# Feed-forward gate and up in a two-block transformer kernel: activations standing against 512 moving weight columns, or weight tiles standing against 512 moving activation columns

## The reference

```python
def rms_norm(x, g):
    y = xf * lax.rsqrt(jnp.mean(xf * xf, axis=-1, keepdims=True) + RMS_EPS)
    return (y * g).astype(x.dtype)

def swiglu(x, w_gate, w_up, w_down):
    return (jax.nn.silu(x @ w_gate) * (x @ w_up)) @ w_down

# first block, once before the mixer and once behind it
f1 = swiglu(rms_norm(x, ffn1_pre_g[l]), ffn1_w_gate[l], ffn1_w_up[l], ffn1_w_down[l])
x = x + FFN_RESIDUAL_WEIGHT * rms_norm(f1, ffn1_post_g[l])
# second block
x = x + (jax.nn.silu(h2 @ w_ffn_gate[l]) * (h2 @ w_ffn_up[l])) @ w_ffn_down[l]
```

## Time and profile before

| | |
|---|---|
| median of three runs | 1033.18 us (1032.8 to 1033.62) |
| the profiled execution, its own time | 1033.55 us |
| span of its trace | 1031.8 us |
| TensorE busy | 1024.5 us, 99% of the span |
| TensorE weight loads busy (beside matmuls) | 849.1 us, 82% |
| VectorE busy | 631.9 us, 61% |
| ScalarE busy | 473.0 us, 46% |
| GpSimd busy | 71.6 us, 7% |
| weights read from HBM | 177.15 MB, 174 GB/s over the span |

### The profile page before, as it was taken

One profiled execution on the slowest core, in us unless ns is written; L12 is line 12 of the kernel. 1 busy time (PEld: TensorE's weight loads), 2 busy tenths in 40 slices (PEclk: granted clock), 3 DMA queues, 4 the chain that ended last, 5 costly groups with the idle time before them and its releaser, 6 DMA issues.

```text
span 1031.8 us, 13503 instructions
## 1 busy us (share of the span) xinstructions
PE 1024.5 (99%) x5002; PEld 849.1 (82%) x5002; DVE 631.9 (61%) x651; ACT 473.0 (46%) x550; POOL 71.6 (7%) x85
## 2 busy tenths in 40 slices
PE   9999999999999999999999999999999999999998
PEld 6888888888878888888888888888888888888887
DVE  6554455765677654454665488876877675445453
ACT  5534345555465534344544442345437354434432
POOL 1000000120100000000010003262000000000000
PEclk9999999999999999999999999999999999999999
DMA  9655556664224555565746653335435646555541
GB/s 307 232 194 189 191 187 211 197 203 128 99 83 163 168 199 185 181 200 183 246 129 199 197 170 97 111 121 164 147 109 193 202 165 205 189 191 188 196 170 41
DMA packets 116665, 178.78 MB, mean 173 GB/s; under 512 B 5641, under 2 KB 73489, under 8 KB 116497
## 3 DMA queue, kind: packets, MB, share of 16 engines
q1 hardware_dynamic: 115808, 174.82, 51.4%
q10 hardware_dynamic: 304, 1.70, 0.6%
q0 software_dynamic: 512, 1.71, 0.6%
HBM read 177.15 MB, written 2.63 MB: 174 GB/s over the span
## 4 chain that ended last, share of the span: by engine, by line
PE 97%; DVE 1%; DMA 1%; issue 0%; ACT 0%; SPq 0%; ACTq 0%; DVEq 0%
PE gu L518 15%; PE gu L522 14%; PE gu L521 14%; PE acc L518 11%; PE acc L522 11%; PE acc L521 11%; PE tp L518 3%; PE tp L522 3%; PE tp L521 3%; PE acc L888 2%; PE tp L658 1%; PE gu L765 1%; PE acc L747 1%; PE acc L777 1%; PE tp L561 1%; DMA raw<-in_up 1%
## 5 line engine op out<-in xcount | busy, mean ns | idle before, releaser
L1568 DVE TENSOR_TENSOR wlo<-raw,whi 128x2048 fp32r<-128x2048 f32 x149 | 346.4, 2328 | 182.6 <-ACT whi L1070 181.8
L1070 ACT ACTIVATE whi<-raw 128x2048 fp32r<-128x2048 f32 x150 | 286.3, 1912 | 141.7 <-PE acc L522 92.8
L518 PE MATMUL gu<-whi,act_hi 128*128 128x512 f32 x592 | 234.8, 397 | 0.1
L522 PE MATMUL gu<-whi,act_lo 128*128 128x512 f32 x592 | 231.0, 390 | 0.0
L521 PE MATMUL gu<-wlo,act_hi 128*128 128x512 f32 x592 | 230.6, 390 | 0.0
L522 PEld LDWEIGHTS gu<-whi,act_lo 128*128 128x128 f32 x592 | 111.1, 188 | 23.7
L518 PEld LDWEIGHTS gu<-whi,act_hi 128*128 128x128 f32 x592 | 111.2, 188 | 23.0 <-DVE act_lo L1594 0.5
L521 PEld LDWEIGHTS gu<-wlo,act_hi 128*128 128x128 f32 x592 | 111.3, 188 | 21.9
L518 PE MATMUL acc<-whi,hT_hi 128*128 128x512 f32 x240 | 93.7, 390 | 0.0
L522 PE MATMUL acc<-whi,hT_lo 128*128 128x512 f32 x240 | 93.4, 389 | 0.0
L521 PE MATMUL acc<-wlo,hT_hi 128*128 128x512 f32 x240 | 93.4, 389 | 0.0
(11 more groups left out here) (275 smaller groups left out, 1342.7 us busy)
## 6 DMA issues: line engine op xcount, KB each, us to landing
raw<-in_w_in SPq DMA_DIRECT2D x96, 512.0 KB, 4.4
raw<-in_down SPq DMA_DIRECT2D x66, 512.0 KB, 3.9
raw<-in_gate SPq DMA_DIRECT2D x64, 512.0 KB, 3.9
raw<-in_up SPq DMA_DIRECT2D x64, 512.0 KB, 4.8
raw<-in_w_out SPq DMA_DIRECT2D x16, 512.0 KB, 4.6
raw<-in_w_branch_hg SPq DMA_DIRECT2D x8, 512.0 KB, 4.2
raw<-in_w_branch_attn SPq DMA_DIRECT2D x8, 512.0 KB, 4.9
post<-in_post_gains SPq DMA_DIRECT2D x3, 512.0 KB, 5.3
```

What stands on the lines that cost most here:

```text
L518: pe.matmul(out, hi, w_hi, start=start, stop=False)
L522: return pe.matmul(out, lo, w_hi, start=False, stop=stop)
L1070: act.activation(split_weights(k)[0], raw[:, k % RING, :], ACT.Copy).then_inc(hi_ready, 1)
L1568: dve.tensor_tensor(w_lo, raw[:, k % RING, :], w_hi.bitcast(F32), ALU.subtract).then_inc(lo_ready, 1)
```

## The change

From chunk 1 on, gate and up are computed the other way round. Chunk 0 stays as it was.

- A piece now holds one of the two matrices for all 1024 inputs (`gate_or_up`). A turn's pieces are gate of chunk c, down of chunk c-1, up of chunk c.
- `act_hi` and `act_lo` lie side by side in `act_in`. A 128x128 tile of w_hi stands and 512 columns move: the 256 tokens of `act_hi` and the 256 of `act_lo` (L694). Then the tile of w_lo stands and 256 columns of `act_hi` move (L695). For each of gate and up that is 2 halves of the features x 8 input tiles x 2 matmuls.
- The result lies with features on partitions and tokens on columns, in two halves of a bank that have yet to be added: VectorE does this with tensor_reduce (gate into `gate`, L1717, which is part of `tmp`; up into `hid`, L1725), two instructions for each matrix.
- `rstd` now varies along the columns. Once per feed-forward TensorE turns it into a row, broadcast over the partitions (`turn_rstd`, two transposes, L683), and ScalarE copies it to `row`. GpSimd multiplies gate's sum by it ahead of the silu and `sil` behind the silu (the `rstd` of up), two instructions each per chunk (L1521 to L1526).
- ScalarE's silu reads `gate` (L1161); VectorE multiplies `hid` by `sil` (L1728).
- `hid` needs no turning. ScalarE copies it rounded to `hT_hi` (L1166), VectorE makes the rest (L1733). The four transposes per chunk go, but for chunk 0.

The core of the diff:

```diff
-        act_hi = sb("act_hi", [P, KT, S], F32R)
-        act_lo = sb("act_lo", [P, KT, S], F32R)
+        act_in = sb("act_in", [P, KT, 2, S], F32R)
+        act_hi, act_lo = act_in[:, :, 0, :], act_in[:, :, 1, :]
...
-            hT_hi, hT_lo = (ffn_part.enter_context(nc.sbuf_tensor(n, [P, 2, S], F32R)) for n in ("hT_hi", "hT_lo"))
+            hT_hi, hT_lo = (ffn_part.enter_context(nc.sbuf_tensor(n, [P, 2, 2, S], F32R)) for n in ("hT_hi", "hT_lo"))
...
+        def hT_place(c):
+            return 1 if isinstance(c, int) and c == NC - 1 else 0
+        gate, row = tmp[:, 0, :].rearrange("p (a n) -> p a n", a=2), tmp[:, 1, 0:S]
+        turned_rstd, turned_hid = acc[:, 1, 0, 0:S], acc[:, 1, 1, :].rearrange("p (a n) -> p a n", a=2)
...
+            def gate_or_up(w, k, r, c):
+                dst = raw[:, k % RING, :].rearrange("p (k n) -> p k n", k=KT)
+                load(k, r, [(dst[:, 4 * a:4 * a + 4, :],
+                             w.rearrange("(k p) n -> p k n", p=P)[:, 4 * a:4 * a + 4, bass.ds(c * FC, FC)])
+                            for a in range(2)])
...
-                def step(k, c, r):
-                    gate_up(f, k, r, c, 0)
-                    gate_up(f, k + 1, r, c, 1)
-                    down(f, k + 2, r, c - 1)
-                step(n0 + 2, 1, 0)
+                gate_or_up(wg_d[f], n0 + 2, 0, 1)
                 if f == 0:
                     sp.dma_start(fixed[:, G_END + P:], fixed_d[:, G_END + P:]).then_inc(fixed_in, 16)
-                with sp.Fori(2, NC) as c:
-                    step(n0 - 1 + 6, c, c - 2)
-                down(f, n0 + 3 * NC - 1, 0, NC - 1)
+                gate_or_up(wu_d[f], n0 + 3, 0, 1)
+                down(f, n0 + 4, 0, 0)
+                with sp.Fori(2, NC - 1) as c:
+                    gate_or_up(wg_d[f], n0 + 5, c - 2, c)
+                    down(f, n0 + 6, c - 2, c - 1)
+                    gate_or_up(wu_d[f], n0 + 7, c - 2, c)
+                k = n0 + 3 * NC - 4
+                gate_or_up(wg_d[f], k, 0, NC - 1)
+                gate_or_up(wu_d[f], k + 1, 0, NC - 1)
+                down(f, k + 2, 0, NC - 2)
+                down(f, k + 3, 0, NC - 1)
...
+                def turn_hidden():
+                    pe.wait_ge(h_ready, h0 + 2)
                     for a in range(2):
-                        for t in tiles:
-                            mm = pe.transpose(tp[:, bank, a * S + t * P:a * S + (t + 1) * P],
-                                              hid[:, t, a * P:(a + 1) * P], idn)
+                        for t in range(TT):
+                            mm = pe.transpose(turned_hid[:, a, t * P:(t + 1) * P], hid[:, t, a * P:(a + 1) * P], idn)
                     mm.then_inc(hT_full, 1)
-                def turn_hidden(c):
-                    pe.wait_ge(h_ready, h0 + 2 + 2 * c)
-                    hidden_to(0, c, range(TT))
+                def turn_rstd():
+                    pe.wait_ge(rstd_ready, norm_n(f"pre{2 * f}", 1))
+                    for t in range(TT):
+                        mm = pe.transpose(turned_rstd[:, t * P:(t + 1) * P], rstd[:, t:t + 1].to_broadcast([P, P]), idn)
+                    mm.then_inc(rstd_turned, 1)
+                def features(k, r, banks):
+                    pe.wait_ge(lo_ready, k + 1 + 3 * r)
+                    w_hi, w_lo = (w.rearrange("p (k n) -> p k n", k=KT) for w in split_weights(k))
+                    for a in range(2):
+                        for i in range(KT):
+                            both = act_in[:, i, :, :].rearrange("p a n -> p (a n)")
+                            pe.matmul(banks[:, a, :], w_hi[:, i, a * P:(a + 1) * P], both, start=i == 0, stop=False)
+                            mm = pe.matmul(banks[:, a, 0:S], w_lo[:, i, a * P:(a + 1) * P], act_in[:, i, 0, :],
+                                           start=False, stop=i == KT - 1)
+                        mm.then_inc(piece_used if a else block_full, 1)
...
-                def of_last(a, t):
...
+                def of_chunk(c):
+                    return lambda a, t: tuple(h[:, hT_place(c), a, t * P:(t + 1) * P] for h in (hT_hi, hT_lo))
+                features(n0 + 2, 0, tp)
+                turn_rstd()
+                turn_hidden()
+                features(n0 + 3, 0, gu)
+                pe.wait_ge(rstd_row, f + 1)
+                pe.wait_ge(hT_lo_ready, t0 + 1)
+                for t in range(TT):
+                    down(n0 + 4, 0, of_chunk(0), True, t)
+                with pe.Fori(2, NC - 1) as c:
+                    pe.wait_ge(gate_sum, s0 + 2 * (c - 1))
+                    features(n0 + 5, c - 2, tp)
+                    pe.wait_ge(hT_lo_ready, t0 + 2 * c - 1)
                     for t in range(TT):
-                        gu_free(c, t)
...
+                        down(n0 + 6, c - 2, of_chunk(c), False, t)
+                    pe.wait_ge(up_sum, s0 + 2 * (c - 1))
+                    features(n0 + 7, c - 2, gu)
                 k = n0 + 3 * NC - 4
-                gu_free(NC - 1, 0)
...
+                pe.wait_ge(gate_sum, s0 + 2 * (NC - 2))
+                features(k, 0, tp)
+                pe.wait_ge(up_sum, s0 + 2 * (NC - 2))
+                features(k + 1, 0, gu)
+                for t in range(TT):
+                    pe.wait_ge(hT_lo_ready, t0 + 2 * NC - 3)
+                    down(k + 2, 0, of_chunk(NC - 2), False, t)
+                    pe.wait_ge(hT_lo_ready, t0 + 2 * NC - 1)
+                    last_down(k + 3, t)
...
+                def silu(c, a):
+                    act.wait_ge(gate_scaled, s0 + 2 * c - 1 + a)
+                    act.wait_ge(h_ready, h0 + 2 * c - 1 + a)
+                    act.activation(sil[:, a, :], gate[:, a, :], ACT.Silu).then_inc(sil_ready, 1)
+                def hidden(c, a):
+                    act.wait_ge(h_ready, h0 + 2 * c + 1 + a)
+                    act.activation(hT_hi[:, hT_place(c), a, :], hid[:, a, :], ACT.Copy).then_inc(hT_hi_ready, 1)
...
+                act.wait_ge(rstd_turned, f + 1)
+                act.activation(row, turned_rstd, ACT.Copy).then_inc(rstd_row, 1)
+                act.wait_ge(hT_full, f + 1)
+                act.activation(hT_hi[:, 0, :, :], turned_hid, ACT.Copy).then_inc(hT_hi_ready, 1)
...
                 with act.Fori(2, NC - 1) as c:
-                    hidden(n0 + 4, c - 2, c - 1)
+                    silu(c, 0)
                     hi(n0 + 8, c - 2)
-                    both(n0 + 6, c - 2, c)
+                    silu(c, 1)
                     hi(n0 + 9, c - 2)
+                    hidden(c, 0)
+                    hidden(c, 1)
                     hi(n0 + 10, c - 2)
-                last = n0 + 3 * NC - 1
-                hidden(last - 4, 0, NC - 2)
-                hi(last)
-                edge_silu(last - 2, NC - 1, 0)
+                hi(n0 + 3 * NC - 1)
+                silu(NC - 1, 0)
                 if n1 is not None:
                     hi(n1)
+                silu(NC - 1, 1)
+                hidden(NC - 1, 0)
+                hidden(NC - 1, 1)
+                if n1 is not None:
                     hi(n1 + 1)
-                edge_silu(last - 2, NC - 1, 1)
-                for t in range(TT):
-                    act.wait_ge(hT_full, h1 + NC + t)
-                    act.activation(last_hT(act_hi, t), heads(tp[:, t, :], 2)[:, :, t * P:(t + 1) * P], ACT.Copy)\
-                       .then_inc(hT_hi_ready, 1)
...
+            def ffn(f):
+                h0, s0 = 2 * f * NC, 2 * f * (NC - 1)
+                pool.wait_ge(rstd_row, f + 1)
+                with pool.Fori(1, NC) as c:
+                    for a in range(2):
+                        pool.wait_ge(gate_sum, s0 + 2 * c - 1 + a)
+                        pool.tensor_tensor(gate[:, a, :], gate[:, a, :], row, ALU.mult).then_inc(gate_scaled, 1)
+                        pool.wait_ge(sil_ready, h0 + 2 * c + 1 + a)
+                        pool.tensor_tensor(sil[:, a, :], sil[:, a, :], row, ALU.mult).then_inc(sil_scaled, 1)
...
+                def gate_parts(k, r, c, a):
+                    if a:
+                        dve.wait_ge(piece_used, k + 1 + 3 * r)
+                    else:
+                        dve.wait_ge(block_full, s0 + 2 * c - 1)
+                    dve.tensor_reduce(gate[:, a, :], tp[:, a, :].rearrange("p (two n) -> p n two", two=2), AX, ALU.add)                       .then_inc(gate_sum, 1)
+                def up_parts(k, r, c, a):
+                    if a:
+                        dve.wait_ge(piece_used, k + 1 + 3 * r)
+                    else:
+                        dve.wait_ge(block_full, s0 + 2 * c)
+                    dve.tensor_reduce(hid[:, a, :], gu[:, a, :].rearrange("p (two n) -> p n two", two=2), AX, ALU.add)                       .then_inc(up_sum, 1)
+                    dve.wait_ge(up_sum, s0 + 2 * c - 1 + a)
+                    dve.wait_ge(sil_scaled, s0 + 2 * c - 1 + a)
+                    dve.tensor_tensor(hid[:, a, :], hid[:, a, :], sil[:, a, :], ALU.mult).then_inc(h_ready, 1)
```

(59 more changed lines are left out.)

94 lines of the change are left out of this document (25 added, 69 removed).

## The result

| | median us | against before (95%) |
|---|---|---|
| before | 1033.4 (4 runs beside it) | |
| the changed kernel | 1047.33 (1046.21 to 1048.61) | 1.0134 [1.0121, 1.0146] |
| forecast | 1036.7, range 1028 to 1050 | slower at 0.57 |

It is slower by 13.9 us, where 3.5 were forecast. The profiled execution took 1048.61 us, 15.1 more than that of before.

The account below looks back on a forecast made before the run. TensorE, busy 99% of the span, was taken as the bound. Transposes -12.8, matmuls +1, holes +13.1, seam +0.8, start +0.2, clock +1.2 sum to +3.5: 1036.7 us from a median of 1033.18, range 1028 to 1050.

Parts of the forecast that it names:

- Transposes, -12.8: TensorE's path: 114 fewer transposes over three feed-forwards, 0.112 us each, come out whole, -12.8 us.
- Matmuls, +1, bounds -3 to +8: Gate and up on TensorE: 256 columns cost half of 512; 1 ns extra on each of 960 short matmuls, +1 us.
- starts off by over 5 ns: Sign set beforehand: forecast wrong if matmul starts on TensorE miss by over 5 ns; short ones expected at 0.113 to 0.115.
- C: Rival, chance 0.05: short matmuls on TensorE are bound by weight loads at 0.122 us, +8 instead of +1, total 1040.
- VectorE and GpSimd: Chunk loop: sums 0.69 us, GpSimd products 0.71, blocking 0.15 to 0.6 per turn; chain 16.3 against TensorE's 16.35, no hole.
- rival A: Chance 0.2: the loop's side-engine chain outlasts TensorE's turn, leaving holes; 1048 with slower sums, 1051 with slower GpSimd.
- Holes, +13.1: End of each feed-forward: TensorE waits for chunk 10's hidden rests, 5.4, 5.4 and 2.3 us, +13.1 in all.
- The clock, +1.2, bounds 0 to 2.4: Behind two long holes TensorE may run at 1.2 GHz; six matmuls lose 0.2 us each, 0 to +2.4, taken 1.2.
- Seam +0.8: Between feed-forwards: the next stage's second piece has its rest 0.4 us late, twice, +0.8 us (0 to +2).
- start +0.2: Beginning of f = 0: the row's copy and gate's sums stand behind setup's VectorE work, +0.2 us (0 to +1).
- Rival B: Chance 0.25: the stall at the feed-forward's end is small; 1028.4 us with half the stalls, 1022 with none.
- my main case: Chance 0.5: the summed terms hold, with stalls of 4 to 6.5 us and clock 0 to 2.4; 1032 to 1042 us.

Follow-up runs that it names:

- e7: Kernel before with one transpose instead of four in chunks 1 to 9 of each feed-forward (81 of 132 left out): 1024.38 us, 0.9917 of before.
- e6: Changed kernel with, per half, eight matmuls of 512 columns and then eight of 256 instead of eight pairs: 1045.37 us, 1.0119 of before.
- e4: Changed kernel with matmuls in the order 512, 512, 256, 256 instead of 512, 256, 512, 256: 1043.14 us, 1.0093 of before.
- e10: Changed kernel with the second matmul of each pair 384 columns wide instead of 256: 1091.37 us, one run.
- e1: Changed kernel with rounding and rest of the next stage's first piece moved behind chunk 10's hidden work: 1040.93 us, 1.0072 of before.
- e5: Changed kernel, tail reordered: chunk 10's gate sums before the last down piece's rest, next stage's first rest behind chunk 10's hidden work: 1036.55 us, 1.0031 of before.
- e2: Changed kernel with 18 unread 512-column matmuls in TensorE's hole before the last down piece of f = 0 and 1: 1043.62 us, 1.0101 of before.

## Why the prediction was right and wrong

The direction was right, and so was the place of the holes; but nearly half of what the kernel lost came from the matmuls, which I had priced at +1, and the sum was 11 us too small (1036.7 against 1047.33).

- *Transposes, -12.8.* Right: e7 prices them at 0.112 on the path.
- *Matmuls, +1, bounds -3 to +8.* The step that failed: "whether 256 columns cost half is seen in the mixer". It was +11.7, and with the slower blocks of down behind it +13.2, beyond my upper bound; by my own sign, starts off by over 5 ns, this part was wrong, since the wide matmul takes 0.236 where I assumed 0.227. I took the slot of 512 as proportional to its columns. It is not: at the half clock the starts are 0.427 us apart, so at the full clock the columns alone would take half of that, 0.2133, and the slot is 0.2268, 0.0135 more. If a matmul of half the width keeps all of it, it takes 0.1067 + 0.0135 = 0.120, which is the steady step of the narrow ones in e6, and two cost 0.347 against 0.3484 and 0.3487 measured in e4 and e6; alternating them brings it to 0.3527. This fits, but a fixed part in every matmul is argued and not shown: the narrow steps range from 0.113 to 0.120, and wide ones pay too. The mixer's rows had the price: 0.116 apart is 0.009 over 0.1067, and the wide matmul ahead of them took 0.24, as it takes 0.236 ahead of a narrow one in the changed kernel. I compared the narrow ones with this slow neighbour instead of with 0.227, and so read them as half. The rival of this term, C, had the sign at a price of its own, loads 0.122 apart. I had misread: the 1.98 us hold a first step of 0.226, and the other loads start 0.112 apart, less than half a slot. e10 excludes a load that does not fit as the whole cost. Whether the load has a part is open: the steady step is 0.120 in e6 beside loads of 128x128, and 0.116 in the mixer beside loads of 128x16.
- *VectorE and GpSimd.* The prices were right, 683 ns for a sum (0.69) and 739 for a product (0.71), and so was the blocking, but not its size: 29 of the 60 products of `sil` began beside a rest and took 2.55 us, 1.8 longer than alone, where I had 0.15 to 0.6 in each turn. The slack in the loop's chain covered it: the chain stayed under TensorE's turn, no hole stands in the loop, and so rival A, whose time of 1048 is near the measured one, did not happen. Its sign, a turn as long as with transposes, came true through the matmuls. A time that fits proves no mechanism.
- *Holes, +13.1.* Right in place and cause, 5.4, 5.4, 2.3 against 4.56, 4.56, 1.52. TensorE arrived 0.6 us later by the slower matmuls, and the halves were ready 0.2 sooner after down(8) than walked. e1 and e5 show that the order of the tail is the cause.
- *The clock, +1.2, bounds 0 to 2.4.* The mechanism was right and shown by e2, the size was not: +5.4. I priced it by the kernel's start, six matmuls of 0.2; behind the hole of f = 0 the starts stayed 0.427 us apart from 191.22 to 196.76, thirteen steps, behind that of f = 1 for eleven. In e6's trace they were five and ten, so this size is not a constant. The sentence on the Trainium skill took its upper end from the same price, and so was short too.
- *Seam +0.8, start +0.2.* Neither came. n1+1's rest was not waited for: e2 needs 9.23 us from the last down piece to the next stage, before 9.20. The first block of down begins at 32.24 us, in before at 32.51.

Rival B (a small stall) fell in the changed kernel. "Slower" was right for a cause that was there, the holes. That the time lies in the range is luck in part: my main case ended at 1042, and the room above it was there for rival A, which did not happen.

## What to carry to other kernels

Half the columns are not half the time: cutting one wide matmul into more and narrower ones with the same columns cost 8 to 12 ns per pair here, and 12 ns on 960 pairs, with what the wide matmuls behind them lost, paid away 114 transposes. A hole of 4.6 to 4.8 us on TensorE cost another 1.4 to 2.9 us through its clock and one of 2.4 us another 1.6, so a tail that leaves it idle should be looked at first, and even useless work in it can pay. When a side engine gets more work, write out its order at the seams, not its busy share.
